# Collecting the expert outputs transposed (features on partitions) instead of token by token, in a one-layer decoder step

## What is computed

```python
x = x + moe(rmsnorm(x, g_ffn), w_router, b_router, w_gate, b_gate, w_up, b_up, w_down, b_down)
gate_p = sigmoid(rmsnorm(x, g_ple) @ w_ple_gate)
x = x + gate_p * (p @ w_ple_proj)
y = rmsnorm(x, g_final)
```

## Time and profile before

| | |
|---|---|
| median of 3 runs | 1276.72 us (1275.2 to 1278.67) |
| the profiled execution, its own time | 1274.7 us |
| its span, first to last instruction | 1273.0 us |
| TensorE busy in the span | 1242.8 us (98%) |
| VectorE, ScalarE, GpSimd busy | 340.0, 172.5, 48.6 us |
| read from HBM | 454.41 MB, 362 GB/s over the span |
| mean granted TensorE clock | 0.998 |

### The profile page before, as it was taken

One profiled execution on the slowest core, in us unless ns is written; L12 is line 12 of the kernel. 1 busy time (PEld: TensorE's weight loads), 2 busy tenths in 40 slices (PEclk: granted clock), 3 DMA queues, 4 the chain that ended last, 5 costly groups with the idle time before them and its releaser, 6 DMA issues.

```text
span 1273.0 us, 15848 instructions
## 1 busy us (share of the span) xinstructions
PE 1242.8 (98%) x6326; PEld 614.1 (48%) x6326; DVE 340.0 (27%) x685; ACT 172.5 (14%) x434; POOL 48.6 (4%) x129
## 2 busy tenths in 40 slices
PE   9999999999999999999999999999999999999996
PEld 7857888855434344343434433333334343434343
DVE  3155445423131213122121303122121212121224
ACT  3136204011101010000001000000000010101013
POOL 2221000200000000000000000000000000000001
PEclk9999999999999999999999999999999999999999
DMA  9947713698999999999999999999999999999961
GB/s 347 287 143 261 273 67 97 238 354 355 417 409 415 422 421 422 420 422 421 422 422 422 422 422 422 422 422 422 422 421 422 422 422 422 422 422 420 421 241 36
DMA packets 79782, 460.98 MB, mean 362 GB/s; under 512 B 8158, under 2 KB 9235, under 8 KB 30842
## 3 DMA queue, kind: packets, MB, share of 16 engines
q1 hardware_dynamic: 74512, 445.18, 85.5%
q0 software_dynamic: 3280, 10.75, 2.7%
q10 hardware_dynamic: 1946, 4.43, 1.0%
HBM read 454.41 MB, written 6.39 MB: 362 GB/s over the span
## 4 chain that ended last, share of the span: by engine, by line
PE 78%; DMA 15%; SPq 5%; DVE 1%; issue 1%; ACT 0%; POOLq 0%; POOL 0%; DVEq 0%
PE bank L1142 29%; DMA arena<-in_w_gate_dram 10%; PE bank L1172 9%; PE bank L704 9%; PE bank L1224 5%; SPq L445 5%; PE bank L746 4%; PE bank L1048 3%; PE bank L685 2%; DMA arena<-in_w_down_dram 2%; DMA arena<-in_w_up_dram 2%; PE bank L1158 2%; PE bank L1058 2%; PE bank L1281 1%; PE bank L1299 1%; PE bank L896 1%
## 5 line engine op out<-in xcount | busy, mean ns | idle before, releaser
L1142 PE MATMUL bank<-arena 128*64 128x512 f32 x2352 | 520.3, 595 | 14.1 <-DMA arena<-in_w_up_dram 7.9
L1142 PEld LDWEIGHTS bank<-arena 128*64 128x64 f32 x2352 | 166.3, 137 | 349.3 <-issue 347.8
L1172 PE MATMUL bank<-arena 128*64 128x512 f32 x720 | 159.1, 595 | 1.0 <-DMA arena<-in_w_gate_dram 1.0
L2061 DVE TENSOR_TENSOR arena<-bank,arena 128x512 f32<-128x512 f32 (+1 forms) x92 | 59.0, 683 | 244.9 <-PE bank L1224 244.6
L704 PE MATMUL bank<-arena 128*128 128x264 f32 x512 | 115.9, 388 | 0.0
L704 PEld LDWEIGHTS bank<-arena 128*128 128x128 f32 x512 | 96.8, 190 | 16.6 <-issue 0.2
L1172 PEld LDWEIGHTS bank<-arena 128*64 128x64 f32 x720 | 51.1, 137 | 107.1 <-issue 107.1
L1048 PEld LDWEIGHTS bank<-arena 128*128 128x128 f32 x512 | 62.8, 196 | 25.4 <-issue 25.2
L1224 PE MATMUL bank<-arena 128*128 128x512 f32 (+1 forms) x192 | 75.0, 602 | 0.0
L2043 DVE TENSOR_SCALAR arena<-bank 128x512 f32<-128x512 f32 x32 | 20.6, 686 | 193.3 <-PE bank L1142 193.3
L2054 DVE COPY arena<-bank 128x512 f32<-128x512 f32 x16 | 11.1, 692 | 223.2 <-PE bank L1142 223.2
(11 more groups left out here) (264 smaller groups left out, 762.9 us busy)
## 6 DMA issues: line engine op xcount, KB each, us to landing
arena<-in_w_gate_dram SPq DMA_DIRECT2D x128, 1024.0 KB, 25.8
arena<-in_w_up_dram SPq DMA_DIRECT2D x128, 1024.0 KB, 26.0
arena<-in_w_down_dram SPq DMA_DIRECT2D x126, 1024.0 KB, 26.1
arena<-in_w_in_dram SPq DMA_DIRECT2D x14, 2048.0 KB, 11.0
out_dram<-arena POOLq DMA_DIRECT2D x9, 512.0 KB, 6.9
arena<-in_state_hgrn_dram POOLq DMA_DIRECT2D x8, 512.0 KB, 8.1
arena<-sample_values ACTq DMA_DIRECT2D x8, 512.0 KB, 8.9
arena<-in_w_out_dram SPq DMA_DIRECT2D x4, 1024.0 KB, 8.0
```

Source lines behind the costliest of these rows:

```text
L1142: ins = pe.matmul(out[c][hp(one), :], src[:, k * P + CAP * one:k * P + CAP * one + CAP], w[one][:, j, halves(c)], start=(first and k == 0) ...
L1172: ins = pe.matmul(GATE[c][hp(one), :], xT_e[:, k * P + CAP * one:k * P + CAP * one + CAP], w[one][:, j, halves(c)], start=False, stop=False)
L2061: ins = dve.tensor_tensor(xs, src, xs, ALU.add)
```

## The change

The running sum over the experts is kept transposed, in `xt`, as eight slices of 128 features x 264 tokens. `mix` now takes a slice k of `y_sb` as the stationary operand and `comb` as the moving one, all 264 tokens at once: eight matmuls of 264 columns into banks 2, 3, 4, 5, 2, 3, 4, 5, where six of 512 columns stood. For the last four TensorE waits until VectorE has taken the slice four before. VectorE makes eight operations of 128x264 per pair in place of four of 128x512 and two of 8x512.

In pair 0 the slices begin with `x` itself: for each k `turn_x1(k)` makes three f32 matmuls with an identity (128, 128 and 8 tokens) into the same bank, ahead of the mix. In pair 1 each mix begins with `down_bias(k)`, one matmul of 32 rows and 264 columns; `down_biases` and `sample_down_biases`, and VectorE's additions of them, are gone.

In pair 15 ScalarE makes `xT` = `xt` x `gple` ahead (all but the last pair's share); VectorE then adds the last share with its gain to `xT` and, in a second operation, without it to `xt`, slice by slice, as the eight mixes come in (banks 2 to 7, 0, 1). `first_gate` starts when the first two slices are in. `xt` is transposed back (`turn_back`, three times eight transposes) between the steps of the gate's product, and VectorE copies it to `xo`, from which the squares and the last sums are taken. The sample rows' `project` moves from pair 15 to pair 14, ahead of the four others, since `xT` now lies over its weights.

```diff
@@ bank_jobs
-    jobs += [(("bd", t, half), 4 + 2 * t + half, "v") for t in range(2) for half in range(2)]
-    jobs += [(("bd2", half), 4 + half, "v") for half in range(2)]
     jobs += [(("pT", k), 6 + k, "a") for k in range(2)]
+    jobs += [(("pp", 2, j), 6, "a") for j in range(4)]
+    jobs += [(("pp", t, half), 4 + half, "a") for t in range(2) for half in range(2)]
     for r in ("", "2"):
...
+        jobs += [(("xr" + r, t, half), (4, 0, 6)[t] + half, "v") for t in ORD[1:2] + ORD[0:1] + ORD[2:3] for half in range(2)]
@@ build
-        pps = [view(HG + 8192, D), view(HG + 9216, D), view(R + 14336, D)]
+        pps = [view(X + t * D, D) for t in range(NT)]
+        xt = heads(HG + 8192)
-        xT = heads(R + 19456)
+        xT = heads(V + HALF)
@@ TensorE
+            def down_bias(k):
+
+                rows = slice(k // 4 * NE, (k // 4 + 1) * NE)
+                pe.matmul(bank[2 + k % 4][:, 0:T], bias_dd[rows, (k % 4) * P:(k % 4 + 1) * P], wT[rows, :], start=True,
+                          stop=False, skip_group_check=True, tile_position=(rows.start, 0))
+
+            def turn_x1(k):
+
+                for t in range(NT):
+                    pe.matmul(bank[2 + k % 4][:, toks(t)], x[lanes(t), t, k * P:(k + 1) * P], ident[lanes(t), lanes(t)],
+                              start=(t == 0), stop=False, skip_group_check=True)
...
-                        if second and m == 1 and g == 0:
-                            pe.wait_ge(s_free45, i + 1)
-                            pe.wait_ge(s_free6, i + 1)
-                            down_biases()
-                        if second and m == 1 and g == 2:
-                            sample_down_biases()
...
                         if project_tiles and m == 1 and g == 0:
                             pe.wait_ge(ld["wproj"], 16)
-                            pe.wait_ge(s_free45, i + 1)
+                            pe.wait_ge(s_mixed, 8 * (i + 1))
+                            project(2, 0)
                         if project_tiles and m == 1:
-                            project("", g // 2, g % 2)
+                            for half in ((), (0,), (1, 2), (3,))[g]:
+                                project(half // 2, half % 2)
...
-                if last:
-                    project("", 2, 0)
-                else:
+                if project_tiles:
+                    wait_drained(pe, ("pp", 2, 3))
+                if not last:
...
-                def mix_half(t, c):
-
-                    out = (UP, AT)[t][c][:, :] if t < 2 else bank[6][32 * c:32 * c + NS, :]
-                    return pe.matmul(out, comb[:, toks(t)], y_sb[:, halves(c)], start=True, stop=True)
...
+                def mix(ks, banks):
+
+                    for k in ks:
+                        out = bank[banks[k]][:, 0:T]
+                        if opening:
+                            turn_x1(k)
+                        if second:
+                            down_bias(k)
+                        pe.matmul(out, y_sb[:, k * P:(k + 1) * P], comb, start=not (opening or second), stop=True,
+                                  skip_group_check=True).then_inc(s_mix, 1)
 
                 if last:
-                    wait_drained(pe, ("pp", 2, 3))
                     pe.wait_ge(s_yhs, 1)
-                    last_mix(0, 0)
+                    mix(range(4), (2, 3, 4, 5, 6, 7, 0, 1))
                     pe.wait_ge(s_ys, 2 * i + 2)
-                    last_mix(0, 1)
-                    finish("", last_mix)
+                    mix(range(4, KD), (2, 3, 4, 5, 6, 7, 0, 1))
+                    finish("")
                 else:
...
-                    mix(0)
-                    mix(1)
-                    pe.wait_ge(s_xe, 2 * i + 3)
-                    mix(2)
+                    mix(range(4), (2, 3, 4, 5))
+                    for k in range(4, KD):
+                        pe.wait_ge(s_mixed, 8 * (i + 1) + k - 3)
+                        mix((k,), (2, 3, 4, 5, 2, 3, 4, 5))
...
+                def turn_back(t):
+                    pe.wait_ge(s_mixed, 8 * (blocks * PAIRS + 1))
+                    for half in range(2):
+                        name = ("xr" + r, t, half)
                         begin(name)
-                        for j, k in enumerate(range(4 * half, 4 * half + 4) if t < 2 else range(KD)):
-                            ins = pe.transpose(job_bank(name)[:, j * n:(j + 1) * n], x[0:n, t, k * P:(k + 1) * P],
-                                               ident[0:n, 0:n])
+                        for j in range(4):
+                            ins = pe.transpose(job_bank(name)[lanes(t), j * P:(j + 1) * P], xt[:, 4 * half + j, toks(t)], ident)
                         fill_done(ins, name)
...
+                        pe.wait_ge(s_xTk, (KD if r else 0) + k + 1)
+                        if k == 0:
+                            pe.wait_ge(s_mixed, 8 * (NBLK * PAIRS + 1) if r else 8 * PAIRS + 2)
...
-                turn(0, (0,))
-                if mix:
-                    mix(1, 0)
-                turn(0, (1,))
                 first_gate(range(4))
-                if mix:
-                    mix(1, 1)
-                    mix(2, 0)
-                    mix(2, 1)
+                turn_back(0)
                 first_gate(range(4, 6))
-                turn(2)
-                turn(1)
+                turn_back(2)
+                turn_back(1)
                 first_gate(range(6, KD))
@@ ScalarE
+            def times_gain(pairs, done):
+
+                act.wait_ge(s_mixed, 8 * (pairs + 1))
+                for k in range(KD):
+                    act.activation(xT[:, k, :], xt[:, k, :], ACT.Copy, scale=gple[:, k:k + 1]).then_inc(done, 1)
...
                 if last:
-                    for j in range(4):
-                        projected("", 2, j)
+                    times_gain(PAIRS - 1, s_xTg)
@@ VectorE
                 if last:
-                    finish("", add_last)
+                    for k in range(KD):
+                        src = bank[(2 + k) % 8][:, 0:T]
+                        dve.wait_ge(s_mix, 8 * i + k + 1)
+                        dve.wait_ge(s_xTg, k + 1)
+                        dve.scalar_tensor_tensor(xT[:, k, :], src, gple[:, k:k + 1], xT[:, k, :], ALU.mult, ALU.add)\
+                           .then_inc(s_xTk, 1)
+                        dve.tensor_tensor(xt[:, k, :], src, xt[:, k, :], ALU.add).then_inc(s_mixed, 1)
+                    finish("")
                 else:
...
+                    for k in range(KD):
+                        src = bank[2 + k % 4][:, 0:T]
+                        dve.wait_ge(s_mix, 8 * i + k + 1)
+                        if first:
+                            ins = dve.tensor_copy(xt[:, k, :], src)
+                        else:
+                            ins = dve.tensor_tensor(xt[:, k, :], src, xt[:, k, :], ALU.add)
+                        ins.then_inc(s_mixed, 1)
+                    dve.wait_ge(s_mixed, 8 * (i + 2))
...
+                def rows_of_x(t):
+                    for half in range(2):
+                        name = ("xr" + r, t, half)
+                        wait_filled(dve, name)
+                        drain_done(dve.tensor_copy(xo[lanes(t), t, halves(half)], job_bank(name)[lanes(t), :]), name)
```

More of the change, by code:

```diff
@@ L177, in build @@
         flag = view(take(1), 1, 1).bitcast(I32)
[L178 removed]
+        FS = take(64)
+        fs = view(FS, 64).rearrange("p (h b) -> p h b", h=H)
         ks = view(take(64), 64).rearrange("p (h b) -> p h b", h=H)
@@ L611, in finish @@
             def finish(r1):
-                for t in range(NT):
-                    pool.wait_ge(s_sq3, 3 * r1 + t + 1)
+                for n, t in enumerate((0, 2, 1)):
+                    pool.wait_ge(s_sq3, 3 * r1 + n + 1)
                     s = stat[lanes(t), 8 + t:9 + t]
@@ L1069, in turn_half, with project @@
                 return ins
-            def project(r, t, n):
-                name = ("pp" + r, t, n)
+            def project(t, n):
+                name = ("pp", t, n)
                 begin(name)
@@ L1348, in _ @@
                 pe.wait_ge(s_xe, 2 * NBLK * PAIRS + 2)
-                pe.wait_ge(s_x3, 2 * NT)
-                for t in range(2):
-                    for n in range(2):
-                        project("2", t, n)
-                project("2", 2, 0)
                 finish("2")
@@ L1572, in finish @@
                 first = 3 if r else 0
[L1574 to L1582 removed]
                 def sum_x(t):
[L1585 to L1588 removed]
+                    wait_drained(act, ("xr" + r, t, 1))
+                    if t != ORD[1]:
+                        act.wait_ge(s_sq3, first + (0, 2, 1)[t])
+                    act.activation(sq[lanes(t)], xo[lanes(t), t, :], ACT.Square, scale=1.0 / 32,
                                    accum_out=stat[lanes(t), 8 + t:9 + t]).then_inc(s_sq3, 1)
@@ L1607, in sum_final @@
                                    accum_out=stat[lanes(t), c:c + 1]).then_inc(s_sqf, 1)
-                turned_x(0)
```

(15 more changed lines are left out.)

143 lines of the change are left out of this document (29 added, 114 removed).

## The result

The changed kernel takes 1283.63 us (median of 5 runs, 1283.12 to 1286.42), the kernel before 1276.14 (5 runs): ratio 1.0062, 95% interval 1.0046 to 1.0079. It is slower by 7.5 us, where 1277.7 and a range up to 1282.5 were forecast. The profiled execution took 1286.42 us with a span of 1284.7, 11.7 more than before.

The account below looks back on a forecast made before the run. The weight stream was taken to bound up to 1114.5 us, TensorE's chain after it. Stream delay +2.4 and end -1.4 gave +1.0 on 1274.7, 1275.7; the median lies 2.0 above, so 1277.7 us, range 1273.5 to 1282.5.

Parts of the forecast that it names:

- What bounds the kernel: Up to 1114.5 us the weight stream at 422 GB/s bounds, behind it TensorE's chain; savings of pairs 2 to 12 worth nothing.
- rival A: Pairs 2 to 14: TensorE's shorter pairs count in full, -7.1 us in all, 1269.6 us; chance 0.04.
- Pair 0: Pair 0's mix: turning x adds 5.5 us, the mix saves 1.0, so everything behind is 4.5 us later (3.8 to 5.4).
- Pair 1: Pair 1: old biases save 1.8 us, eight down-bias matmuls cost 3.6; TensorE is 5.3 us late behind its mix.
- The stream: Weight reads behind the mixes of pairs 0 and 1: issued late into a thin queue, delay 2.4 us (0 to 6.2).
- the queue arithmetic of the forecast: Early reads: landing time less the shortest, 4.8 us, is work in front (1.8 behind pair 0); lateness beyond it empties the DMA.
- No second gap: Behind pair 1's mix: 9.4 + 2.4 - 5.3 = 6.5 us to landing, over 4.8, so the stream does not empty again.
- rival C: Stream empty behind the mixes of both pairs 0 and 1: up to +4.8 us, 1281.5 us; chance 0.14.
- The end: TensorE's path behind 1114.5 us: -2.0 + 1.0 - 1.1 + 0.7 = -1.4 us (-2.4 to 0).
- rival D: Kernel end: rows turned back delay tile 0's squares, `pow` and sigmoid, 1 to 2 us onto the end, 1279.2; chance 0.1.

Follow-up runs that it names:

- the bunched run: Changed kernel with x turned in pair 8 and pair 1's 32-row matmuls four in a row ahead of four mixes; ratio 1.0009 to the kernel before.
- with it alone: Changed kernel with only the down biases moved, from pair 1's mix to pair 9's, x still turned in pair 0; ratio 1.0044 to the kernel before.
- the second comparison: Changed kernel, unaltered, run and profiled again against the kernel before: 1283.84 us against 1275.62, ratio 1.0063.
- the load put there: Kernel before plus matmuls of 256 columns that nobody reads, 16 and 9, ahead of the mixes of pairs 8 and 9; ratio 1.0022.

## Why the prediction was wrong

**What bounds the kernel** was right: the eleven shorter mixes in pairs 2 to 12 (3.76 us each for 4.59) gave nothing, against rival A, and the time moved with the delay of the weight stream.

**The failing step** is the pair "Pair 0" and "Pair 1", terms of the lateness. I took 0.26 us for a full turning matmul and 0.447 for every matmul of 264 columns, from runs of one form, and 0.16 for the turning one of 8 rows, between two bounds. The three turning ones of a slice then make 0.68 us and the mix 0.45. In alternation they cost 0.85 and 0.55, and in pair 1 both kinds cost 0.64. TensorE was 6.8 us late behind pair 0's mix (77.5 us from pair 0's first product, 70.7 before) where I had 4.5 (my own upper end was 5.4), and 10.5 behind pair 1's where I had 5.3. For pair 1 the bunched run shows that the order is most of it, not the 32 rows: there both kinds take 0.50 us. This agrees with what the forecast cited from the Trainium skill, "TensorE: Matmul & The Clock Gate", section "Why this matters for your kernels", that 32 rows take the time of 128.

**The stream** then followed the queue arithmetic of the forecast to within 0.7 us a hole. With the measured lateness it gives 6.8 - 1.8 = 5.0 us for the first hole (5.7 measured with it alone). Behind pair 1 it gives 9.4 + 5.0 - 10.5 = 3.9 us to landing, which is less than the 4.8 that a read takes, so a second hole of 0.9 (1.6 measured). "No second gap" was wrong because of the 5.3 in it. Together that is 7.3 us measured, 5.9 by the arithmetic and 2.4 in the forecast. So 3.5 of the 4.9 us missing in this term come from the lateness. The other 1.4 come from holes that were longer than the arithmetic makes them, and why is open. What happened is rival C, whose place was right and whose price, 6.2 us at most, was made with the same low prices; it had 0.14.

**The end** was forecast at -1.4 and is -2.0: 156.5 us for 158.5 where the clock stays full. The mixes of pairs 13 and 14 save 0.83 each and not 1.01, and the sample rows' project costs the 0.98 that I had. From the last mixes' start to the last run of gate products it is 20.1 us for 21.2, where I had 0.4 less. The other products of the embeddings in pair 14 take 7.45 us for 7.65. VectorE was never late for `first_gate`, and the rows turned back held up nothing (rival D).

**The clock** was not in the forecast at all. The changed kernel's runs had a mean of 0.9943 in the second comparison, the kernel before 0.9957: 2 x 0.0014 x 1280 = 3.6 us more at 1.2 GHz, 1.8 us if on the path, and 1.4 by the line through the runs of the kernel before. 7.3 - 2.0 + 1.4 = 6.7 us, against 7.5 and 8.2 measured in the two comparisons; 0.8 and 1.5 us stay open.

**The range.** Its upper end was built on the same low lateness: no queue at all and still only 6.2 us of delay. Yet the lateness alone would not have taken the time out of it. With 6.8 and 10.5 us in place of 4.5 and 5.3, the forecast's own arithmetic gives 5.9 - 1.4 = +4.5, or 1281.2 us. The longer holes and the clock are the rest of the way to 1283.63.

## What to carry to other kernels

In a kernel bound by a stream of transfers, look for the stretch where the least is queued, and compare the time from issue to landing there with the shortest one seen. Their difference is about all the lateness that the consumer may have (the holes here came out 0.7 us longer than it says). One-time work belongs some pairs later, where the queue has grown: moved to pairs 8 and 9, it lengthened the stream by 0.1 us, and the load put there by 0.4. Take the price of a short matmul from a place where it alternates as it will in the new code; if the trace has only uniform runs, leave room for it in the range (the two mixes here were 25% and 42% longer than priced), and bunch matmuls of one shape where banks allow.

## What the hardware showed that I had not expected

- f32 matmuls of 264 columns: 0.447 us each in a long uniform run, 0.47 as eight mixes, 0.50 in fours of one shape, 0.55 behind the turning ones, and 0.64 in turn with a 32-row one.
- The granted clock of a single core fell to 1.2 GHz for some 3 to 10 us at a time, at places that differ between executions of one program: ahead of pair 0, behind the wait in pair 15, once in the mix of alternating 32-row matmuls, where TensorE had not waited for 9 us. Runs of the kernel before at 0.998 took 1274 us and at 0.993 some 1279, a spread wider than most effects here; a comparison of two profiles has to take those places out first.
